# Mixing loop of a hybrid encoder block: one of six projection units moved out of the preparation and into the solve, which gives up two accumulator banks for it

## What is computed

```python
h = rmsnorm(x, mix_norm)
q, k, v, z_rwkv, gate_a, gate_b = _split(h @ w_in, IN_SIZES)
zr, zk, zv, uw, ua, ug = _split(token_shift_mix(z_rwkv, mu), RWKV_SHIFT_SIZES)
o_a = window_gqa_sinks(q, k, v, sinks)
...
def step(state, inp):                       # o_b: per head of 64, over all tokens
    r_t, w_t, k_t, v_t, a_t, b_t = inp
    sa = einsum('bhvk,bhk->bhv', state, a_t)
    state = state * w_t + sa[..., None] * b_t + v_t[..., None] * k_t
    return state, einsum('bhvk,bhk->bhv', state, r_t)
...
merged = sigmoid(gate_a) * o_a + sigmoid(gate_b) * o_b
x = x + merged @ w_out
```

## Time and profile before

| what | us |
|---|---|
| median of 3 runs | 3308.3 |
| lowest, highest | 3306.97, 3312.1 |
| the profiled execution | 3300.46 |
| span in its trace | 3298.7 |
| mixing loop in it | about 1150, from about 900 to 2050 |
| one middle iteration | 70.4 |

### The profile page before, as it was taken

The page is one execution under the profiler, slowest core; times in us unless marked ns, Lnnn a source line. Parts: engine busy times, 40 slices in busy tenths (PEclk is TensorE's granted clock), DMA queues, the critical chain, the costliest instruction groups (busy, mean ns, idle before and its releaser), DMA issues. The chain is left out here.

```text
span 3298.7 us, 61271 instructions
## 1 busy us (share of the span) xinstructions
PE 2941.7 (89%) x26974; PEld 2437.3 (74%) x26974; DVE 1682.8 (51%) x1907; ACT 993.2 (30%) x1542; POOL 1216.4 (37%) x603
## 2 busy tenths in 40 slices
PE   3899999996899999999999986797976799999995
PEld 2688888884688877788877765786755588887884
DVE  6654444444176666667666763113222744453445
ACT  2433333222233333333333421212221333333221
POOL 1444444442354433454443430222131344444441
PEclk7999999997999999999999997898988899999997
DMA  3222224433221111322111100611002122234441
GB/s 140 82 94 80 80 103 166 144 121 134 60 66 54 52 46 45 98 63 60 52 46 46 47 24 12 222 59 32 19 26 89 64 80 77 77 102 166 144 144 67
DMA packets 247429, 270.71 MB, mean 82 GB/s; under 512 B 13184, under 2 KB 204800, under 8 KB 245120
## 3 DMA queue, kind: packets, MB, share of 16 engines
q1 hardware_dynamic: 247168, 266.84, 24.5%
HBM read 218.57 MB, written 48.23 MB: 81 GB/s over the span
## 5 line engine op out<-in xcount | busy, mean ns | idle before, releaser
L460 POOL TENSOR_TENSOR w_low<-ffn_work,w_high 128x1024 fp32r<-128x1024 f32 x182 | 445.4, 2448 | 667.4 <-ACT w_high L533 394.2
L500 PE MATMUL bank<-h_high,w_high 128*128 128x512 f32 x1232 | 484.9, 394 | 57.2 <-DVE h_low L644 35.9
L500 PE MATMUL bank<-h_high,w_low 128*128 128x512 f32 x1232 | 483.4, 392 | 0.0
L500 PE MATMUL bank<-h_low,w_high 128*128 128x512 f32 x1232 | 483.4, 392 | 0.0
L691 DVE TENSOR_TENSOR h_low<-ffn_work,h_high 128x512 fp32r<-128x512 f32 x88 | 204.3, 2321 | 250.6 <-ACT h_high L548 250.6
L1076 POOL TENSOR_TENSOR mix_panel_low<-arena,mix_panel_high 128x1024 fp32r<-128x1024 f32 x96 | 240.6, 2506 | 233.5 <-ACT mix_panel_high L1426 233.4
L1164 PE MATMUL bank<-mix_h_high,mix_panel_high 128*128 128x512 f32 x768 | 312.3, 407 | 13.8 <-POOL mix_panel_low L1076 13.6
L500 PEld LDWEIGHTS bank<-h_high,w_high 128*128 128x128 f32 x1232 | 234.2, 190 | 109.6 <-issue 57.5
L1164 PE MATMUL bank<-mix_h_high,mix_panel_low 128*128 128x512 f32 x768 | 300.2, 391 | 0.0
L1164 PE MATMUL bank<-mix_h_low,mix_panel_high 128*128 128x512 f32 x768 | 300.1, 391 | 0.0
L517 PE MATMUL bank<-h_high,w_high 128*128 128x512 f32 x704 | 274.8, 390 | 4.5 <-DVE h_low L691 4.5
(11 more groups left out here) (261 smaller groups left out, 5667.0 us busy)
## 6 DMA issues: line engine op xcount, KB each, us to landing
arena<-w_in SPq DMA_DIRECT2D x96, 512.0 KB, 3.7
ffn_work<-w_down SPq DMA_DIRECT2D x88, 512.0 KB, 3.6
a_spill<-ffn_work SPq DMA_DIRECT2D x88, 256.0 KB, 2.2
ffn_work<-a_spill SPq DMA_DIRECT2D x88, 256.0 KB, 2.6
ffn_work<-w_gate SPq DMA_DIRECT2D x12, 1024.0 KB, 5.5
ffn_work<-w_up SPq DMA_DIRECT2D x12, 1024.0 KB, 8.1
arena<-x_spill SPq DMA_DIRECT2D x3, 4096.0 KB, 13.9
arena<-w_gate SPq DMA_DIRECT2D x10, 1024.0 KB, 5.4
```

Source lines behind the costliest of these rows:

```text
L460: nc.gpsimd.tensor_tensor(slot(w[1], q), src, slot(w[0], q).bitcast(F32), ALU.subtract).then_inc(s_low, 1)
L500: last = mm(bank[:, bk, :], w[wp][:, q % RING, kt, e], h[hp][:, k, kt], start=fresh and kt + wp + hp == 0, stop=kt == KT // 2 - 1 and wp = ...
```

## The change

Unit 5 of iteration i+1 leaves `prepare(i)`. On PE it is cut into five pieces of 4, 5, 5, 5 and 5 products, which stand in `solve(i)` behind the growth of q = 0 and the chain step of each level, ahead of the growth of q = 1. It accumulates in P1, so the growths of both halves now share F0 (xt) and F1 (x), and the growth of q = 1 waits until DVE has added that of q = 0. On ACT the store and the rounding, on POOL the subtraction, that go with unit 5 now follow the whole of `solve(i)`. The wait for the last xt_added moves ahead of the low-rank products of `prepare`, whose banks are F0 and F1.

```diff
@@ banks
-            ZB, TB, XB = (F2, F3), (P0, P1), (F0, F1)
+            ZB, TB, XB = (F2, F3), F0, F1
@@ POOL: prepare, then the loop
-                        for j in range(3, NP):
+                        for j in range(3, NP - 1):
                             next_panel(i, j)
...
                         if i < ITER:
                             solve(i)
+                        next_panel(i, NP - 1)
@@ PE: project
-                    def project(unit):
-                        if unit >= UNITS:
-                            return
-                        pe.wait_ge(S("panel_low"), unit + 1)
-                        if unit >= 2:
-                            pe.wait_ge(S("proj_stored"), unit - 1)
...
+                    def project(unit, first=0, end=TERMS):
+
+                        if first == 0:
+                            pe.wait_ge(S("panel_low"), unit + 1)
+                            if unit >= 2:
+                                pe.wait_ge(S("proj_stored"), unit - 1)
+                        for term in range(first, end):
+                            kt, (wp, hp) = term // 3, THREE[term % 3]
...
+                            last = mm(bank[:, unit % 2, :], pw[wp][:, unit % 2, kt], hA[hp][:, kt],
+                                      start=term == 0, stop=term == TERMS - 1)
+                        if end == TERMS:
+                            last.then_inc(S("proj_ready"), 1)
@@ PE: prepare
                             pe.wait_ge(s_lora, 48 * i + 48)
+                            if i > 0:
+                                pe.wait_ge(S("xt_added"), 10 * i)
...
                         if more:
-                            if i > 0:
-                                pe.wait_ge(S("xt_added"), 10 * i)
                             project(first)
...
                             project(first + 4)
-                            project(first + 5)
@@ PE: score slots 3 and 5
-                                    pe.wait_ge(S("proj_stored"), NP * (i + 2))
+                                    pe.wait_ge(S("proj_stored"), NP * (i + 1) + 4)
...
+                                if i + 1 < ITER:
+                                    pe.wait_ge(S("proj_stored"), NP * (i + 1) + 5)
                                 scores(P0, k_ch, 1).then_inc(S("k_scores_ready"), 1)
@@ PE: growths
-                                    seen("x_added", 8, 2 * n - 1 + q)
+                                    seen("x_added", 8, 2 * n)
+                                if q == 1:
+                                    seen("xt_added", 10, 2 * n + 1)
+                                    if n < 4:
+                                        seen("x_added", 8, 2 * n + 1)
...
-                                    grown = to_other(one(TB[q])[:, m, :], x_st[:, at, :], z_st[:, at, :])
+                                    grown = to_other(one(TB)[:, m, :], x_st[:, at, :], z_st[:, at, :])
@@ PE: the loop over slots
                             if step:
                                 chain_step(*step)
+                            if live and i + 1 < ITER and s >= SCORES and quarter(s)[1] == 2:
+                                n = quarter(s)[0]
+                                if n == 0:
+                                    seen("b_tok_stored")
+                                project(NP * (i + 2) - 1, n * TERMS // 5, (n + 1) * TERMS // 5)
@@ ACT: prepare, then the loop
                         next_unit(4)
-                        next_unit(5)
...
                         if i <= ITER:
                             solve(i)
+                        if i + 1 < ITER:
+                            store(NP * (i + 2) - 1)
+                            round_panel(NP * (i + 2) + 1)
```

More of the change, by code:

```diff
@@ L1152, in heads @@
                         return last
-                    def project(unit):
-                        if unit >= UNITS:
-                            return
-                        pe.wait_ge(S("panel_low"), unit + 1)
-                        if unit >= 2:
-                            pe.wait_ge(S("proj_stored"), unit - 1)
-                        for kt in range(KT):
-                            if unit == NP * PAIRS:
+                    def project(unit, first=0, end=TERMS):
[5 more added lines that the diff above has]
+                            kt, (wp, hp) = term // 3, THREE[term % 3]
+                            if unit == NP * PAIRS and term % 3 == 0:
                                 pe.wait_ge(s_half[kt], 32)
-                            for wp, hp in THREE:
-                                last = mm(bank[:, unit % 2, :], pw[wp][:, unit % 2, kt], hA[hp][:, kt],
-                                          start=kt + wp + hp == 0, stop=kt == KT - 1 and wp == 1)
-                        last.then_inc(S("proj_ready"), 1)
+                            last = mm(bank[:, unit % 2, :], pw[wp][:, unit % 2, kt], hA[hp][:, kt],
+                                      start=term == 0, stop=term == TERMS - 1)
+                        if end == TERMS:
+                            last.then_inc(S("proj_ready"), 1)
                     def prepare(i):
@@ L1355, in level_slot @@
                                     if n < 4:
-                                        last = heads(one(XB[q])[:, m, :], z_st[:, at, :], x_st[:, at, :])
+                                        last = heads(one(XB)[:, m, :], z_st[:, at, :], x_st[:, at, :])
                                 if n < 4:
@@ L1398, in solve @@
                                 score_slot(s)
-                            elif live and quarter(s)[1] < 2:
-                                level_slot(*quarter(s), beside=step)
-                                continue
                             elif live:
-                                level_slot(*quarter(s))
+                                beside = step if quarter(s)[1] < 2 else None
+                                level_slot(*quarter(s), beside=beside)
+                                if beside:
+                                    continue
                             if step:
                                 chain_step(*step)
+                            if live and i + 1 < ITER and s >= SCORES and quarter(s)[1] == 2:
[3 more added lines that the diff above has]
+                                project(NP * (i + 2) - 1, n * TERMS // 5, (n + 1) * TERMS // 5)
                         if back:
@@ L1722, in level_slot @@
                                     seen("xt0_ready", 2, q + 1)
-                                V.tensor_tensor(part(xt_new, q), one(TB[q])[:, 0:4], part(xt_new, q),
+                                V.tensor_tensor(part(xt_new, q), one(TB)[:, 0:4], part(xt_new, q),
                                                 ALU.add).then_inc(S("xt_added"), 1)
@@ L1728, in level_slot @@
                                         seen("x_added", 8, 2 * n - 1 + q)
-                                    V.tensor_tensor(part(x_st, q), one(XB[q])[:, 0:4], part(x_st, q),
+                                    V.tensor_tensor(part(x_st, q), one(XB)[:, 0:4], part(x_st, q),
                                                     ALU.add).then_inc(S("x_added"), 1)
```

8 lines of the change are left out of this document (2 added, 6 removed).

## The result

| | before | changed |
|---|---|---|
| median, us | 3308.5 | 3334.7 |
| lowest, highest, us | 3307.0, 3312.1 | 3330.7, 3338.1 |
| the profiled execution, us | 3300.46 | 3330.65 |
| ratio to before | | 1.0076, 95% interval 1.0063 to 1.0089 |

The forecast was 3325, slower, in a range of 3302 to 3347. The time is inside and the sign is right; the change costs 26 us where the sum had 17. (The four executions of before, at 3307.0, 3308.3, 3308.7 and 3312.1, have their median at 3308.5; the profiled one, 3300.46, is not among them.)

A forecast was written before the change was run, and what follows sets the result against it. PE bounds the preparation, a serial PE, ACT, DVE chain the solve. Solves +5, preparations +8, half switch +2, solve 15 +2: +17 us on 3300.46, or 3325 on the median 3308.3; range 3302 to 3347.

The forecast's parts named there:

- the half switch: Second half's load, released late in solve 6: next preparation +6.3 us, solve 6 -4.3, together +2 (0 to +6), once.
- What the preparation gives: PE in the preparation: removing unit 5's 24 products gains 5.45 us in each of 15 iterations.
- What the pieces cost: PE in the solve: five pieces cost 6.5 us, 0.7 hidden, so each solve grows 5.8 us (5.3 to 6.5).
- The shared banks: Growth of q = 1: wait for DVE's additions covered by pieces, 0; uncovered in iteration 15, +2 us once (0 to 4).
- ACT, POOL and the next preparation: Joint of solve and preparation: late POOL and DVE stall PE 0.65 us (0 to 1.3), in 12 iterations.
- one of the prediction's own signs of being wrong: In the changed kernel's trace: DVE or a panel holding PE up by more than 1 us would show the prediction wrong.
- The chain is not the bound: Rival, solve: pieces fill PE's idle time, solve grows only 3.6 us, total 3290 us; chance 0.10.
- The lateness arrives whole: Rival, preparation: PE stalls 2.3 us each time instead of 0.65, +37 us, total 3345; chance 0.15.
- No change: Rival: no preparation stalls and half-price changeovers, or solves growing 5.8 us: +2 to +9, say 3313 us; chance 0.25.

The follow-up runs named there:

- the run with the banks alone: Kernel before with only the shared growth banks, unit 5 and the orders of ACT and POOL unmoved: 3346.6 us, one execution.
- the run with rotating banks: Changed kernel, pieces where they are, bank roles rotating so no growth of q = 1 waits for an addition: 3326.8 us, one execution.
- the run without it: Changed kernel, with POOL's unit 5 panel subtraction moved behind the next preparation's small copy and three differences: 3322.0 us, ratio 1.0043 to before.
- the last run: Changed kernel, but in iteration 6 alone unit 5 stays in the preparation on PE, ACT and POOL: 3334.4 us, one execution.
- one piece behind step 3.2: Changed kernel with rotating banks and unit 5's 24 products in one piece behind step 3.2: 3302.5 us, one execution.
- three pieces: Changed kernel with rotating banks, POOL's subtraction behind the three differences, three pieces of 8 behind steps 2.2, 3.2 and 6.2: 3279.3 us, ratio 0.9914 to before.
- six pieces: Changed kernel with rotating banks and six pieces of 4 behind steps 1.2, 2.2, 3.2, 4.2, 5.2 and 6.2: 3281.2 us, ratio 0.992 to before.
- one piece behind step 2.0: Changed kernel with rotating banks and unit 5's 24 products in one piece behind step 2.0: 3318.8 us, one execution.

## Why the prediction was right, and where its sum was short

Its terms against the two traces, from iteration 0 to the end of the mixing loop:

| term | forecast | measured |
|---|---|---|
| iterations 2 to 14 without 6 and 7 (11 of them) | +11 | +14.5 |
| iteration 1 | +0.4 | +2.2 |
| iterations 6 and 7, with the half switch | +3.4 | +4.6 |
| iteration 0 | 0 | +0.7 |
| iteration 15 to the end of the loop | +2 | +3.8 |
| sum | +17 | +26 |

**What the preparation gives.** Right. 43.33 to 37.9 us when POOL is out of the way is 5.4; the forecast was 5.45.

**What the pieces cost.** The mechanism was right, the size of one term was off. The price of a changeover was put at 0.21 us from the first product behind each change of kind; the runs give 0.31 to 0.40. Five times the missing 0.1 to 0.2 is 0.5 to 1.0; the solve grew by 6.48 instead of 5.8. What hides, forecast as 0.7 for all five, fits: 5.45 + 5 x 0.37 - 6.48 = 0.8 (0.5 to 1.0 by the bounds of the price). In solve 0, which has no chain, nothing hides: its levels grew from 12.50 to 18.63, 6.1 us, and iteration 0 lost 0.7, where the forecast was 0 or a gain of up to 5. The piece behind step 4.2 did swallow its gap, as forecast. Step 4.2 is at 1308.24 and step 5.0 at 1310.47, 2.23 us apart where the earlier trace rows have 1.20, so five products and a changeover, 1.13 + 0.31 to 0.40, cost 1.03 and 0.4 to 0.5 of them are hidden; step 5.0 follows the last products of the growth without a wait:

```profile
1310.41 0.22 PE L1152 MATMUL bank<-arena 64*64 64x64 f32 x2
1310.47 0.28 PE L1152 MATMUL bank<-mix_work,arena 64*64 64x64 f32 x4
```

**The shared banks.** Right: 0 in the steady iterations. The price where nothing covers the wait was a little under-rated: iteration 15 was to pay 2, and its levels grew by 2.7 (20.05 to 22.71); without pieces every solve pays some 2.5. The other 1.2 of the 3.8 in the table are no matter of banks. In the scores of solve 15, before and then changed, the granted clock differs:

```profile
1981.58:1989.80 8.22, 8.21 (x257) 8.22 (x259) 6.36 (x10) 3.00 (x7) 2.43 (x2) 1.00 0.09 34
2002.98:2012.86 9.88, 9.88 (x259) 9.88 (x262) 6.03 (x10) 3.12 (x7) 2.36 (x2) 0.82 0.07 28
```

The same products took 1.66 us longer at 0.82, part of them at the lower of the clock's two levels; the preparation ahead of them was 0.46 shorter. The rule from the Trainium skill ("Perfetto Trace Analysis", section "Matmuls"), that independent groups should rotate through banks, is what the run with the banks alone shows, 2.5 us in a solve; that a piece of other work covers it is what the run with rotating banks shows.

**ACT, POOL and the next preparation.** The story held in each step. POOL was through with the panel at E + 3.2 (forecast 3.3), DVE's first mix ended at E + 6.0 (6.3), DVE's copy was caught behind POOL's subtraction, and PE stalled 0.49 in the row and 0.68 by the run without it (0.65). What was forgotten is iteration 1: its preparation has no output part, and the sum gave it no stall, but it lost 1.8 us, which the run with POOL's order gave back. There PE did wait for a panel, up to 1.1 us at once, one of the prediction's own signs of being wrong; it came true in this one iteration.

**The half switch.** Prepare 7 took 44.44 us against 37.93 in the last run, where the load comes early and no late subtraction stands ahead: 6.5 us (forecast 6.3). Solve 6 got rid of the 4.2 us that the load had cost it, but for 0.3. The net is 2.6 where 2 was forecast, and the last run shows the cause.

**What the sum left out.** The kernel before isn't as regular as its best iterations. Its levels lie between 18.85 and 20.42 us, solve 6 aside, 0.46 over the shortest in the mean, and part of this is idle time of PE for which the profile names no cause ("issue": 4.2 us in iterations 3 to 13, 2.9 of it in solve 6, against 0.4 in the changed kernel); those of the changed kernel agree within 0.05, solve 6 aside. So the +1.74 us between the shortest iterations is +1.32 in the mean. What the "issue" gaps are is told in the last section; the rest of the irregularity is unexplained. Behind the mixing loop the profiled execution loses another 4.5 us, which the medians (26 us apart) don't have.

**The rivals.** "The chain is not the bound" had the right prize and the wrong condition: it let the solve grow by 3.6, and with pieces in the chain's gaps it grew by 3.4; where the change put them it grew by 6.5. The Trainium skill's rule on interleaving stretches with different bounds ("Perfetto Trace Analysis", section "Optimization Strategy") holds here with that condition added: 26 us lost behind the growths, 27 won in the gaps (3281.2 against 3308.7), with the same products. (The second kernel also rotates its banks, which changed the steady levels by under 0.1 us.) "The lateness arrives whole" fell: 0.68 us arrived, except in iteration 1. "No change" needed both cheaper changeovers and no stall, and had neither.

## What to carry to other kernels

Filler in a stretch that a serial chain bounds must stand inside a wait of the chain, behind the step that hands over to the other engine and ahead of the one that then waits, not merely somewhere in the stretch. PE's idle time stayed at 2.8 us with five pieces, of which only the one behind step 4.2 stood so, and fell to 0.7 with six that all did. A gap takes up more than the idle time shown: read its room from the starts of instructions. Follow a moved piece's helpers too: one subtraction on POOL, listed ahead of three operations that the next stage needed, cost 0.68 us in each iteration, and moving it behind them gave it back.

## What the runs showed of the hardware that I had not expected

**A gap holds more than its idle time.** The profile shows 0.74 us idle ahead of step 4.0 in the changed kernel, but PE's last start ahead of it, in the group that begins in the first row, is 0.96 us earlier:

```profile
1305.57 0.28 PE L1285 MATMUL bank<-arena 64*64 64x64 f32 x3
1306.58 0.27 PE L1152 MATMUL bank<-mix_work,arena 64*64 64x64 f32 x2 [0.74 <-DVE mix_work L1759]
```

The products' lengths overlap, so a start can follow a start after 0.06 us, and the last length counts as busy. Measured so, from start to start less 0.06, the six gaps in a shortest solve of the kernel before have 0.35, 0.69, 0.87, 0.49, 0.35 and 0.69 us, 3.4 in all, where the idle times sum to 2.5. The one piece behind step 3.2 hid 0.89: its gap has 0.87 by the starts and 0.71 by the idle time. The three pieces hid 18.85 + 5.45 + 3 x 0.31 to 0.40 - 22.67 = 2.6 to 2.8, of 2.25 by the starts and 1.8 by the idle times; the six pieces 4.0 to 4.5, of 3.4 and 2.5. The starts come nearer in all three cases, but with more pieces they fall short too; where the rest hides is open.

**A large load takes time from PE without any wait for its data.** With unit 47 finished early in solve 6 (one piece behind step 2.0, rotating banks) the load of the second half runs beside the levels. They took 32.4 us instead of 24.7. The stretch:

```profile
1363.17:1395.58 32.41, 25.03 (x702) 22.20 (x700) 12.36 (x36) 4.64 (x17) 0.00 (x0) 0.84 0.46 157
```

PE's longest waits in it:

```profile
PE bank L1155 <- issue: 5.0, 2, 2.7
```

The DMA share is 0.46 instead of 0.02, and PE stands still twice, 5.0 us in all, for nothing that the profile names. In the kernel before solve 6 has two such gaps, the 1.52 of the earlier trace rows and one of 1.36 ahead of it. With the load in prepare 7 instead, as in the changed kernel, the levels of solve 6 are 25.6.

The clock doesn't make the gaps. It is 0.84 in this stretch, so part of it ran at the lower of the two levels, 1.2 GHz, but it fell each time behind a gap: at 1382.0 and 1388.9, where the gaps end at 1381.8 and 1388.2. With the piece behind step 3.2 both gaps lie at full clock.

What ends them stands in the traces of the DMA queues: packets of 16 KB in the queue that the profile calls "q8 instruction". The kernel before has five of them in the levels of solve 5 (first row), this run six in the stretch above (second row):

```profile
q8 instruction: 5, 0.08, 2.0%
q8 instruction: 6, 0.10, 1.2%
```

| run | PE's gap, us | it ends at | last packet landed at | start of that packet after the one ahead of it |
|---|---|---|---|---|
| before | 1.36 | 1368.84 | 1367.56 | 6.4 |
| before | 1.52 | 1374.08 | 1372.70 | 5.1 |
| one piece behind 2.0 | 2.71 | 1381.84 | 1380.36 | 10.3 |
| one piece behind 2.0 | 2.28 | 1388.24 | 1387.02 | 6.5 |
| one piece behind 3.2 | 1.53 | 1378.33 | 1376.88 | 9.3 |
| one piece behind 3.2 | 2.95 | 1385.16 | 1383.91 | 6.9 |

In the levels of solve 5 of the kernel before these packets follow each other in 3.5 to 3.9 us. All 14 traces together have 43 gaps of over 0.25 us between 1000 and 1955 us that the profile puts down to "issue", and in every one such a packet landed 1.2 to 1.6 us before PE went on; of PE's 610 other gaps over 0.4 us only 59 lie so. That speaks for PE waiting there for its next instructions, which come late above all beside the load. No run was made to test it.

**A DVE copy with one operand is held up by POOL too.** It took 2.59 us beside a POOL subtraction and 0.41 without. The prediction had assumed so, but its rows showed it only for operations with two operands in SBUF. The trace of the kernel before had shown it as well: its copy L1628, of the same size, took 2.12 us beside an operation of POOL.
